# Dealing the second mixer's weight slots out to the attention and mLSTM units, and 512-column high-weight matmuls in three channel-major projections

## The reference, cut to what matters

```
h = rmsnorm(x, w);  z = h @ w_in
fq, fk, fv, ff, mq, mk, mv, mi, mf, mo = split(z)
att  = forgetting_attention(fq, fk, fv, ff + bias)       # 8 heads of 128, softmax with a decay
mqk  = silu(causal_depthwise_conv(concat(mq, mk)))        # 4 taps
cell = sigmoid(mo) * mlstm_chunkwise(mq_c, mk_c, mv, mi, mf)  # 4 heads, 2 chunks of 128 tokens
x = x + concat(head_rmsnorm(att), head_rmsnorm(cell)) @ w_out
x = x + peer_ffn(rmsnorm(x))     # q = x @ w_q chooses 16 of 16384 experts per head
```

## Time and profile before

| what | value |
|---|---|
| time, median of 3 runs | 3375.82 us (3375.22 to 3376.74) |
| time of the profiled execution | 3373.92 us |
| its span, first to last instruction | 3372.1 us |
| mean granted clock of PE | 0.942 of 2.4 GHz |
| PE busy | 3111.4 us, 92% |
| DVE busy | 1715.3 us, 51% |
| ACT busy | 1256.4 us, 37% |
| HBM read | 530.68 MB, 160 GB/s over the span |

### The profile page before, as it was taken

The page is one execution under the profiler, slowest core; times in us unless marked ns, Lnnn a source line. Parts: engine busy times, 40 slices in busy tenths (PEclk is TensorE's granted clock), DMA queues, the critical chain, the costliest instruction groups (busy, mean ns, idle before and its releaser), DMA issues.

```text
span 3372.1 us, 49234 instructions
## 1 busy us (share of the span) xinstructions
PE 3111.4 (92%) x20215; PEld 2848.9 (84%) x20215; DVE 1715.3 (51%) x2326; ACT 1256.4 (37%) x1376; POOL 39.3 (1%) x31
## 2 busy tenths in 40 slices
PE   7999998889998698984979999989999999999997
PEld 6999987778997598853879999988888999988885
DVE  4444353444244444646446998864444444444444
ACT  3333343444133333332333334433433333333443
POOL 0400000000000000000000000000000000000000
PEclk9999977889999899965989999999999999999998
DMA  4545443223454344510534445545555755545554
GB/s 176 180 180 187 162 159 115 76 76 123 151 184 165 112 176 173 190 47 9 191 125 162 175 165 171 171 153 187 190 196 187 259 202 187 176 171 188 188 197 150
DMA packets 89849, 542.17 MB, mean 161 GB/s; under 512 B 9264, under 2 KB 25648, under 8 KB 25904
## 3 DMA queue, kind: packets, MB, share of 16 engines
q1 hardware_dynamic: 71824, 522.33, 43.8%
q10 hardware_dynamic: 17952, 18.88, 1.6%
HBM read 530.68 MB, written 10.49 MB: 160 GB/s over the span
## 4 chain that ended last, share of the span: by engine, by line
PE 81%; DVE 11%; ACT 5%; issue 1%; DMA 0%; ACTq 0%; DVEq 0%; SPq 0%
PE bank L424 41%; PE bank L766 21%; PE bank L451 11%; DVE wlo L1255 4%; ACT whi L802 2%; PE bank L589 2%; PE bank L493 2%; DVE R L1742 1%; DVE R L1239 1%; PE bank L547 1%; PE bank L518 1%; PE bank L652 0%; ACT R L836 0%; DVE R L1737 0%; DVE hTl L1231 0%
## 5 line engine op out<-in xcount | busy, mean ns | idle before, releaser
L1255 DVE TENSOR_TENSOR wlo<-raw,whi 128x2048 fp32r<-128x2048 f32 x476 | 1091.3, 2294 | 921.4 <-ACT whi L802 920.4
L424 PE MATMUL bank<-hTh,whi 128*128 128x256 f32 x4480 | 1304.1, 291 | 38.1 <-DVE wlo L1255 36.5
L424 PE MATMUL bank<-hTl,whi 128*128 128x256 f32 x4480 | 1278.4, 285 | 0.0
L424 PE MATMUL bank<-hTh,wlo 128*128 128x256 f32 x4480 | 1278.0, 285 | 0.0
L802 ACT ACTIVATE whi<-raw 128x2048 fp32r<-128x2048 f32 x476 | 907.6, 1909 | 892.6 <-PE bank L424 628.6
L424 PEld LDWEIGHTS bank<-hTh,whi 128*128 128x128 f32 x4480 | 872.4, 195 | 41.7 <-DVE wlo L1255 37.9
L424 PEld LDWEIGHTS bank<-hTl,whi 128*128 128x128 f32 x4480 | 871.3, 194 | 0.0
L424 PEld LDWEIGHTS bank<-hTh,wlo 128*128 128x128 f32 x4480 | 869.9, 194 | 0.0
L766 PE MATMUL bank<-whi,ghi 128*128 128x512 f32 x1024 | 281.6, 397 | 15.3 <-DVE wlo L1255 15.3
L766 PE MATMUL bank<-wlo,ghi 128*128 128x512 f32 x1024 | 276.1, 392 | 0.0
L766 PE MATMUL bank<-whi,glo 128*128 128x512 f32 x1024 | 275.0, 390 | 0.0
(11 more groups left out here) (268 smaller groups left out, 1905.7 us busy)
## 6 DMA issues: line engine op xcount, KB each, us to landing
raw<-stream SPq DMA_DIRECT2D x492, 1024.0 KB, 4.8
gates_dram<-R ACTq DMA_DIRECT2D x64, 128.0 KB, 3.8
R<-gates_dram ACTq DMA_DIRECT2D x16, 512.0 KB, 5.2
xres<-x SPq DMA_DIRECT2D x1, 2048.0 KB, 7.7
out<-R SPq DMA_DIRECT2D x1, 2048.0 KB, 6.4
R<-mixw ACTq DMA_DIRECT2D x1, 1024.0 KB, 4.9
R<-fnw ACTq DMA_DIRECT2D x1, 1024.0 KB, 4.8
raw<-fnw SPq DMA_DIRECT2D x1, 1024.0 KB, 6.0
```

Source lines behind the costliest of these rows:

```text
L424: last = mm(bank[b][:, t * T:(t + 1) * T], w[t][:, ks], x_[:, k, :], start=(k == 0 and n == 0), stop=(k == KC - 1 and n == 2))
L1255: V.tensor_tensor(wlo[t][:], raw[t][:], whi[t][:].bitcast(F32), ALU.subtract).then_inc(raw_free[t], 1)
```

## The change

Two things are changed. First, in `in_t`, `in2_t` and `wq` the activations' high and low parts lie side by side in one tile `hT2`, and one matmul of 512 columns multiplies the high weights with both; the low weights keep their 256 columns. Each slot now fills a bank of its own, whose two halves DVE adds on the way to `R` (`tensor_reduce`); ACT no longer evacuates these phases. Second, the stream is reordered: fv comes right after `narrow2` (`in2_v`, 2 groups), and the slots of mq, mk (`in2_m`, 8 slots) and mv, mo (`in2_n`, 16 slots) are dealt out by the list `MIX`: slots 0 to 3 around the mixer's start, and one slot in each unit, slots 4 to 19 in the 16 attention units and 20 to 23 in the first four mLSTM units. Convolutions move into attention units 5 to 12, their silu to unit 13, the state matmuls into the mLSTM units 0 to 3, and the sigmoid of mo behind the mLSTM units.

```diff
-          ("out1", 4), ("in2_t", 6), ("narrow2", 0.5), ("in2_n", 6), ("out2", 4), ("wq", 4),
+          ("out1", 4), ("in2_t", 4), ("narrow2", 0.5), ("in2_v", 2), ("in2_m", 2), ("in2_n", 4), ("out2", 4), ("wq", 4),
+MIX = [("in2_m", i, s) for i in range(2) for s in range(RING)] + [("in2_n", g, s) for g in range(4) for s in range(RING)]
+MIX_FIRST = 4
+CONV_UNIT = 5
...
-        hTh = sb("hTh", [P, KC, T], F32R)
-        hTl = sb("hTl", [P, KC, T], F32R)
+        hT2 = sb("hT2", [P, KC, 2, T], F32R)
+        hTh, hTl = hT2[:, :, 0, :], hT2[:, :, 1, :]
...
+            def phase_t2(name):
+                with pe.Fori(0, G0[name][1]) as i:
+                    for s in range(RING):
+                        t = s % 2
+                        pe.wait_ge(bank_free[s], i + B0[name][s])
+                        pe.wait_ge(raw_free[t], consumed(name, i, s))
+                        for k in range(KC):
+                            ks = slice(k * P, (k + 1) * P)
+                            both = (bank[s][:], whi[t][:, ks], hT2[:, k, :, :].rearrange("p a t -> p (a t)"))
+                            if k == 0:
+                                mm(*both, start=True, stop=False)
+                            last = mm(bank[s][:, 0:T], wlo[t][:, ks], hTh[:, k, :], start=False, stop=False)
+                            if k > 0:
+                                last = mm(*both, start=False, stop=(k == KC - 1))
+                        last.then_inc(slot_used[t], 1)
+            def mix_slot(n):
+                if n < len(MIX):
+                    name, i, s = MIX[n]
+                    (t_slot if name == "in2_m" else pair_slot)(name, i, s)
...
-            phase_n("in2_n")
+            phase_n("in2_v")
+            for n in range(2):
+                mix_slot(n)
...
             fox_scores(0)
             fox_scores(1)
+            for n in range(2, MIX_FIRST):
+                mix_slot(n)
             for u in range(units):
                 fox_turn(u)
                 if u + 2 < units:
                     fox_scores(u + 2)
+                mix_slot(u + MIX_FIRST)
                 fox_values(u)
...
             for u in range(units):
                 m_turn(u)
                 if u + 2 < units:
                     m_sc(u + 2)
+                if u < MH:
+                    m_state(u)
+                elif u == MH:
+                    pe.wait_ge(bank_free[0], B0["out2"][0])
+                    pe.wait_ge(bank_free[1], B0["out2"][1])
+                mix_slot(MIX_FIRST + FH * TB + u)
                 m_values(u)
...
+                def evac_one(i, s):
+                    dve.wait_ge(slot_used[s % 2], multiplied(name, i, s))
+                    V.tensor_reduce(R[:, bass.ds(i * (4 * T) + s * T, T)], bank[s][:].rearrange("p (a t) -> p t a", a=2),
+                                    AX.X, ALU.add).then_inc(bank_free[s], 1)
+
                 def evac(i, s):
-                    if s == 2:
-                        dve.wait_ge(slot_used[1], multiplied(name, i, 1))
-                        V.tensor_copy(R[:, bass.ds(i * (4 * T), 2 * T)], bank[0][:]).then_inc(bank_free[0], 1)
+                    if s > 0:
+                        evac_one(i, s - 1)
+                    if s == 3:
+                        evac_one(i, 3)
...
             fox_exp(0)
+            mix_split(MIX_FIRST)
             for u in range(units):
+                mix_split(u + MIX_FIRST + 1)
+                mix_evac(u + MIX_FIRST - 1)
+                fox_copy(u)
                 if u + 1 < units:
                     fox_exp(u + 1)
-                fox_copy(u)
+                if u == CONV_UNIT + 8:
+                    act.wait_ge(conv_done, 8)
+                    A(conv, conv, ACT.Silu).then_inc(conv_silu, 1)
...
             fox_mask(0)
+            mix_split(MIX_FIRST)
             for u in range(units):
+                mix_evac(u + MIX_FIRST - 1)
+                if u >= 1:
+                    fox_out(u - 1)
                 if u + 1 < units:
-                    if u >= 1:
-                        fox_out(u - 1)
                     fox_mask(u + 1)
+                mix_split(u + MIX_FIRST + 1)
+                if 0 <= u - CONV_UNIT < 8:
...
+                    convolve(u - CONV_UNIT)
```

More of the change, by code:

```diff
@@ L129, in fills_per_bank @@
 def fills_per_bank(name, n):
-    if name in ("in_t", "merge", "nsa_out", "in2_t", "wq", "peer_u0", "peer_u1"):
+    if name in ("in_t", "in2_t", "wq"):
+        return (n,) * 4
+    if name in ("merge", "nsa_out", "in2_m", "in2_n", "peer_u0", "peer_u1"):
         return (n, n, 0, 0)
-    if name in ("in_n", "out1", "in2_n", "out2"):
+    if name in ("in_n", "out1", "in2_v", "out2"):
         return (n // 2,) * 4
@@ L669, in _ @@
             pe.wait_ge(f_oread, units)
+            pe.wait_ge(q_ready, 2)
+            for h in range(MH):
+                last = nc.tensor.transpose(bank[7][:, h * P:(h + 1) * P], conv[:, 4 + h, 0:P], ident)
+            last.then_inc(knat_ready, 1)
             def m_sc(u):
@@ L844, in evac_t @@
             def evac_t(name):
[L846 to L850, removed]
+                phase(name, keep)
             def phase_n(name, dst, between=None):
@@ L998, in gate_rows, with mix_split, mix_evac @@
                     A(rows[0:4, 5, :], rows[0:4, 5, :], ACT.Ln, bias=1.0).then_inc(row_l, 1)
[L999 to L1004, removed]
+            phase_n("in2_v", vN2, gate_rows)
+            def mix_split(n):
+                if n < len(MIX):
+                    split(*MIX[n])
+            def mix_evac(n):
+                if n < len(MIX):
+                    name, i, s = MIX[n]
+                    if s == 3:
+                        act.wait_ge(slot_used[1], multiplied(name, i, 3))
+                        if name == "in2_m":
+                            A(pT[:, MQ0 + 4 * i + 2:MQ0 + 4 * i + 4, :], bank[1][:].rearrange("p (j t) -> p j t", t=T),
+                              ACT.Copy).then_inc(bank_free[1], 1)
+                        else:
+                            A(vN2[:, 2 + i, 0, :], bank[0][:], ACT.Copy).then_inc(bank_free[0], 1)
+            mix_split(0)
+            mix_split(1)
+            act.wait_ge(a_ready, 1)
+            A(rows[0:4, 11, 0:P], rows[0:4, 9, 0:P], ACT.Exp, bias=rowst[0:4, 1:2]).then_inc(rows_ready, 1)
+            mix_split(2)
             act.wait_ge(nat_ready, 1)
             A(natc[:, 0:36], bank[4][:, 0:36], ACT.Copy).then_inc(nat_copied, 1)
[L1007 to L1011, removed]
+            mix_split(3)
             def fox_exp(u):
@@ L1524, in _ @@
[L1524 to L1533 removed]
+            evac_n("in2_v", vN2, gate_rows)
@@ new lines, in mix_split, with mix_evac @@
+            def mix_split(n):
+                if n < len(MIX):
+                    split(*MIX[n])
+            def mix_evac(n):
+                if n < len(MIX):
+                    name, i, s = MIX[n]
+                    if name == "in2_m" and s == 1:
+                        dve.wait_ge(slot_used[1], multiplied(name, i, 1))
+                        V.tensor_copy(pT[:, MQ0 + 4 * i:MQ0 + 4 * i + 2, :],
+                                      bank[0][:].rearrange("p (j t) -> p j t", t=T)).then_inc(bank_free[0], 1)
+                    if name == "in2_n" and s == 3:
+                        dve.wait_ge(slot_used[1], multiplied(name, i, 3))
+                        V.tensor_copy(vN2[:, 2 + i, 1, :], bank[1][:]).then_inc(bank_free[1], 1)
```

134 lines of the change are left out of this document (90 added, 44 removed).

## The result

The changed kernel takes **3322.0 us** (median of four runs, 3320.3 to 3324.0) beside 3375.5 us of the kernel before: ratio 0.9842, 95% interval [0.9825, 0.9859]. That is 53.5 us faster, where 69.6 were forecast.

What follows compares the result with a forecast made beforehand. PE bounds `in2_t` and `in2_n`, a chain of handoffs the attention and mLSTM stretch. Savings of 20.3 + 3.4 + 45.9 = 69.6 us turn 3373.9 into 3304.3, plus 1.9 for the median: 3306 us, range 3290 to 3332.

Steps and rivals of the forecast that it cites:

- the likeliest case: Whole kernel: the forecast itself, 3306 us with its own range of 3296 to 3318 us; chance 0.62.
- the first rival: 512-column phases: the wide matmul saves nothing, a piece still takes 359.7 ns, 3326 us; chance 0.12.
- The reading of the slices: Old kernel's profile: slices 17 and 18, 84 us each, are the deepest hole, PE 4 tenths busy.
- Part 1, the surcharge of 13.2 ns: `in_t`, `in2_t`, `wq`: each wide matmul saves one 13.2 ns surcharge per piece, 20.3 us over 96 slots.
- Evacuation by DVE's reductions: Wide phases: four DVE reductions per group, 0.69 us each, stay hidden by PE's slot.
- Two handovers of 3.1 us: Ends of `in_t` and `in2_t`: the handover falls from 4.8 to 3.1 us, saving 3.4 us together.
- The handover behind `in2_v`: Before the first dealt slot: a new 4.8 us gap plus 2.6 lost to the fallen clock, 7.4 us added.
- Attention units at 1.46 us each: 16 attention units: PE's own work at full clock, chains hidden under slots, 23.4 us; bounds 1.46 and 3.37 each.
- The second rival: Attention and mLSTM units: chains stay in series with the slots, 41 us more, 3347 us; chance 0.12.
- mLSTM units and tail: Four mLSTM units with a slot add 8.4 us; four without, ending the stretch, add 24.0 us.
- The slower rival: Units with slots: low half comes only after the same unit's DVE outputs and masks; 3403 us, chance 0.03.
- The better case: Handovers and last four mLSTM units: clock stays up, 14 us less, 3292 us; chance 0.08.

Runs made afterwards that it cites:

- Experiment 3: Changed kernel with each slot's sixteen 512-column matmuls grouped ahead of its sixteen 256-column ones; 3309.4 us, ratio 0.9808.
- experiment 1: Changed kernel with the wide matmul taken back to two of 256 columns, DVE's reductions and the mixer kept; 3332.4 us, ratio 0.9877.
- Experiment 5: Changed kernel with ACT copying the finished group's bank before splitting the next slot, in attention and mLSTM units; 3312.0 us, ratio 0.9818.
- Experiment 7: Changed kernel with two weight slots ahead of the attention units instead of four; 3323.2 us, ratio 0.9841.
- experiment 6: Changed kernel with the first dealt slot split before the last evacuation of `in2_v`, on ACT and DVE; 3311.8 us, ratio 0.9812.
- experiment 4: Changed kernel with a slot's matmuls ordered wide, narrow, narrow, wide, wide and so on, in pairs of equal width; 3311.8 us, ratio 0.9811.

## Why the prediction was right, and where it was off

The direction and the mechanism of the mixer held; the time is 16 us above the forecast. It lies inside the wide range, 3290 to 3332 us, but above the likeliest case's own, 3296 to 3318, and only 4 us from the 3326 of the first rival. So the number alone would have spoken for that rival, with the mixer as forecast; that the range held owes something to its having been stretched to take the rival in. What tells the two apart are the pitches. By the steps:

- **The reading of the slices.** Only slice 18 of the old kernel has 4 tenths busy; slice 17 has 8. The sum was made from the windows, so nothing hangs on it.
- **Part 1, the surcharge of 13.2 ns.** This is the first term that was mis-sized: "both pure streams show the same surcharge", so one surcharge was to go per piece. It measured 96 x 0.113 = 10.8 us, half of 20.3. The step from two pure streams to an alternation of them was not in any row. The forecast had named that and took the upper end of its bounds; the truth lay in the middle. Experiment 3 shows that the premise itself was good: with each width in a stream of its own, 96 x (5.760 - 5.567) = 18.5 of the 20.3 us are there. The first rival (nothing saved) fell, by experiment 1.
- By the Trainium skill (TensorE: Matmul & The Clock Gate, Back-to-back issue gap), whose gap of N/2.4 + 2.5 ns is stated there for an isolated matmul, one matmul fewer saves 2.5 ns, an estimate of 3.8 us in all by that page's figure. The runs have 7.1 ns a piece when the widths alternate (360.0 - 352.9, a sixteenth of 5.760 and 5.647 us) and 12.1 when they are grouped, and disagree. For the kernel as changed the 10.8 us lie between the two figures and are nearer to the page's 3.8 than to the forecast's 20.3; for the grouped order, 18.5 us, the forecast by the rows is the nearer.
- **Evacuation by DVE's reductions.** Right: 0.69 us, covered by PE's slot; experiment 1 has them too and keeps the old pitch.
- **Two handovers of 3.1 us.** Right: 2.98 us shown behind `in2_t`, from start to start 1.7 us less at both.
- **The handover behind `in2_v`.** Right in both parts, 4.90 us of wait and 2.5 lost to the half clock (the first two slots' matmuls take 13.94 us from first start to last, at the full pitch 95 x 0.120 = 11.4). The queue on DVE behind it did as said: PE's first slot covers it.
- **Attention units at 1.46 us each.** This is the second term that was mis-sized: 29.3 us instead of 23.4. The full clock was right. What failed was "against it: the copy has a 5.4 us slot to run under". For attention's own copies that held. It was not held against the copy of a finished group of slots, which shares ACT with the split, is released by the same event as the split, and is queued behind it; the next slot writes the same bank, so it has no cover beyond the unit's own PE work of 1.5 us. Experiment 5 removes just that order, and the waits with it. The second rival (everything in series, 41 us) did not come; its mechanism did, at three places of sixteen, for a tenth of its price.
- **mLSTM units and tail.** Right within 0.7 us. The tail of four units still costs 23.5 us with a window clock of 0.64.
- **The slower rival** (low half behind the same unit's outputs) did not come: no wait on `wlo` inside the units. Experiment 7 shows how near it stands: with two slots fewer ahead, one such wait of 3.3 us appears at the first unit.
- **The better case** needed the clock to stay up behind the handovers. After the wait of 2.98 us behind `in2_t` it didn't: some 3 us at half clock follow. That it can, where the gap goes, is shown by experiment 6.

## What to carry to other kernels

- When work is dealt into the waits of a chain, list for each engine what one event releases, and order by who needs it first: here a 0.6 us copy behind a 1.9 us split cost PE 1.4 us each time, and with the copy first the split's slot still had 3.5 us to spare.
- A pitch measured in a stream of equal matmuls holds for streams of equal matmuls. If two widths must be mixed, group them: the same instructions took 5.647 us a slot alternating and 5.567 grouped.
- At a change of phase, split the next phase's first tile before the last tile of this one is evacuated: the gap goes, and the clock's fall with it. Slots placed ahead of a chain are its cover too, so moving them behind it can give back all that it wins.

## What the runs showed of the hardware

- A 512-column matmul between two of 256 columns costs more than in a stream of its own: a wide and a narrow one together 352.9 ns (a sixteenth of a slot), grouped 347.9, in pairs of equal width 348.3, by the two pure pitches 346.5. The cost doesn't follow the number of changes; its cause is open.
- A gap of 5.3 us of PE brought a stretch at 1.2 GHz behind it, with 0.41 us matmuls, and the same code without the gap had none. The waits of 2.98 us (behind `in2_t`, new kernel), 3.3 and 2.0 us (experiment 7) were followed by half clock too. Waits of 1.4 us went both ways: behind unit 8's, the new kernel keeps starts 0.23 us apart, but in experiments 3 and 4 the same wait is followed by half clock, which costs 1.7 us more. Experiment 3:

```profile
1394.04 0.53 PE L472 MATMUL bank<-whi,hT 128*128 128x512 f32 x1 [1.35 <-ACT R L1075]
...
1395.46 1.05 PE L472 MATMUL bank<-whi,hT 128*128 128x512 f32 x2
...
1396.74 1.05 PE L472 MATMUL bank<-whi,hT 128*128 128x512 f32 x2
```

  Pairs of matmuls take 1.05 us there and 0.62 at the full clock. So a small wait's price can be more than its length; what decides it was not found.
- The mean granted clock of the profiled executions was 0.952 to 0.956 with nearly the same code. In stretches where PE is never idle, a thousandth of a span of 3312 us is 3.3 us, so by this estimate such stretches alone can move a run by as much as the smallest effects sought here.
